# A hybrid decoder kernel: a new order of the first loads, block 0 in two passes, products on zeros, one mixing table

## The reference, cut to what matters

```
h = rmsnorm(x)
[u | v | p | q | gate_logits] = h @ w_in
A: a = gelu(u) * (tril(W_s[g]) @ LN(gelu(v)) + b_s[g])   per chunk of 128 rows, 4 groups g
B: b = scale * groupwise_linear(mean over trailing 2, 4, 8, 16 rows of p, minus p)
C: 4-head attention of q into 256 memory tokens
merged = sig(g_A)*P_A(a) + sig(g_B)*P_B(b) + sig(g_C)*P_C(c);  x += merged @ w_o
x += relu(rmsnorm(x) @ w_up)^2 @ w_down;  final rmsnorm
```

## Time and profile before

| | |
|---|---|
| median of three runs | 967.74 us (967.2 to 967.82) |
| profiled execution, its time | 966.78 us |
| span of its slowest core (core 5) | 965.1 us |
| spans of the eight cores | 962.2 to 965.1 us |
| TensorE busy | 910.6 us, 94% of the span |
| VectorE, ScalarE, GpSimd busy | 383.4, 306.4, 276.8 us |

### The profile page before, as it was taken

How to read it: one execution, slowest core, us unless ns; L and a number is a source line. 1 busy time by engine, 2 the same in 40 slices (tenths; PEclk the granted TensorE clock), 3 DMA queues, 4 the chain that set the end, 5 groups by cost and what they waited for, 6 DMA issues and landing times.

```text
span 965.1 us, 15404 instructions; the slowest of 8 cores (962.2 to 965.1 us)
## 1 busy us (share of the span) xinstructions
PE 910.6 (94%) x5196; PEld 466.3 (48%) x5196; DVE 383.4 (40%) x633; ACT 306.4 (32%) x536; POOL 276.8 (29%) x276
## 2 busy tenths in 40 slices
PE   1599999999999999999999999999999999999996
PEld 0265655444455555554455444554445544455442
DVE  0466665423332233335832244223442234322576
ACT  1254674676322222222333200331003310033332
POOL 1123341623343333442433200232003310033243
PEclk9999999999999999999999999999999999999998
DMA  8627246903284222219570220504114050220134
GB/s 157 182 67 186 87 84 116 175 1 47 43 228 78 44 44 45 44 58 247 98 133 1 48 41 1 88 1 66 22 17 72 1 88 1 39 49 1 45 153 175
DMA packets 34060, 74.14 MB, mean 77 GB/s; under 512 B 19887, under 2 KB 20910, under 8 KB 30144
## 3 DMA queue, kind: packets, MB, share of 16 engines
q0 software_dynamic: 5472, 35.65, 22.2%
q1 hardware_dynamic: 28512, 37.51, 12.5%
HBM read 94.24 MB, written 10.22 MB: 108 GB/s over the span
## 4 chain that ended last, share of the span: by engine, by line
PE 89%; DMA 4%; DVE 2%; ACT 2%; issue 1%; POOL 0%; DVEq 0%; SPq 0%; POOLq 0%; ACTq 0%
PE bank L347 88%; DMA X<-x 3%; DMA CR<-ck 1%; PE bank L350 1%; DVE X L365 1%; ACT X L353 1%; ACT L353 1%; ACT fA L353 0%; DVE stats L562 0%; DVE X L362 0%; POOL stats L356 0%; ACT hT L369 0%; DVEq L128 0%; ACT CR L353 0%; SPq L159 0%
## 5 line engine op out<-in xcount | busy, mean ns | idle before, releaser
L347 PE MATMUL bank<-hT,slot 128*128 128x436 bf16 (+3 forms) x2480 | 466.2, 347 | 4.9 <-DVE hT L371 2.0
L347 PEld LDWEIGHTS bank<-hT,slot 128*128 128x128 bf16 x2480 | 238.9, 98 | 218.6 <-issue 8.7
L347 PE MATMUL bank<-slot,CR 128*128 128x512 bf16 (+1 forms) x1376 | 296.3, 378 | 0.0
L353 ACT ACTIVATE fA<-bank 128x436 f32<-128x436 f32 (+2 forms) x215 | 115.6, 545 | 339.5 <-PE bank L347 329.3
L347 PEld LDWEIGHTS bank<-slot,CR 128*128 128x128 bf16 x1376 | 134.5, 98 | 160.4
L365 DVE SCALAR_TENSOR_TENSOR X<-bank,stats,X 128x512 f32<-128x512 f32 x136 | 102.0, 750 | 119.8 <-PE bank L347 119.8
L353 ACT ACTIVATE fW<-bank 128x436 f32<-128x436 f32 (+2 forms) x103 | 54.7, 534 | 166.3 <-PE bank L347 163.8
L356 POOL TENSOR_TENSOR CR<-fA 128x436 bf16<-128x436 f32 (+1 forms) x69 | 67.5, 980 | 106.9 <-ACT fA L353 102.9
L356 POOL TENSOR_TENSOR stats<-stats,cstt 128x1 f32<-128x1 f32 (+3 forms) x32 | 39.6, 1239 | 136.1 <-DVE stats L362 93.8
L356 DVE TENSOR_TENSOR CR<-fA 128x436 bf16<-128x436 f32 (+1 forms) x51 | 32.7, 645 | 114.6 <-ACT fA L353 114.6
L356 DVE TENSOR_TENSOR fA<-bank,fA 128x436 f32<-128x436 f32 (+1 forms) x77 | 42.7, 603 | 78.4 <-PE bank L347 75.2
(11 more groups left out here) (93 smaller groups left out, 490.6 us busy)
## 6 DMA issues: line engine op xcount, KB each, us to landing
slot<-wpk POOLq DMA_DIRECT2D x30, 1024.0 KB, 13.2
X<-x SPq DMA_DIRECT2D x34, 512.0 KB, 7.5
y<-hT SPq DMA_DIRECT2D x17, 512.0 KB, 2.7
CR<-ck POOLq DMA_DIRECT2D x4, 512.0 KB, 9.9
CR<-cv POOLq DMA_DIRECT2D x4, 512.0 KB, 12.1
CR<-mem SPq DMA_DIRECT2D x2, 512.0 KB, 11.0
gb<-gvec SPq DMA_DIRECT2D x2, 512.0 KB, 10.9
fW<-wst SPq DMA_DIRECT2D x2, 256.0 KB, 10.7
```

What stands on the lines that cost most here:

```text
L347: s.op("pe", lambda e: e.matmul(out, lhsT=lhsT, rhs=rhs, start=start, stop=stop), R_, W_)
L353: s.op("act", lambda e: e.activation(out=out, in_=in_, func=func, **kw), R_, W_)
```

## The change

What it does: (1) constants `onef`, `nhalf`, `qbd`, `ones` are set by VectorE; `nhalf` is no longer loaded. (2) The gain row and the identity are issued by ScalarE's queue; tiles 0 and 1 by SyncE's, tiles 2 and 3 by GpSimd's, ahead of the weights. (3) Chunks v, pq and u are loaded as two halves (k = 0 to 3, k = 4 to 7), each with its own semaphore, one behind the other on GpSimd's queue; u is issued after T(0). (4) `cst` is issued once the second half of v has landed, then the window tables, and the setup loads once the first half of pq has landed; tiles 4 to 7 and 8 to 11 now go through GpSimd's queue. (5) Products on zeros, 6, 5 and 4 of 512 columns, stand in TensorE's list around T(0) and T(1). (6) In block 0 V, P, Q and U are done in two passes, all with k = 0 to 3 and then k = 4 to 7, over open banks. (7) The first of block 1 is reordered, and the rows of tiles 4 to 7 are squared between the products of U(0, g). (8) There is one table CC: the K=1 products are gone, b_s comes broadcast over 128 partitions and is added by VectorE, and the second `setup_mm` is gone.

```diff
+        def load_halves(expect):
+            ...
+            for a in range(2):
+                s.dma("pool", [(slots[sl][:, a * 2048:(a + 1) * 2048], wpk[CH[nm]][:, a * 2048:(a + 1) * 2048])],
+                      writes=[slot_b[sl][a]], owner=slot_b[sl][a])
...
-        norm_load(0, xrow(0))
-        s.dma("sp", [(grow, gvec[0].unsqueeze(0))], writes=grow_b, owner=grow_b[0])
-        load_next("v")
-        load_next("pq")
-        load_next("u")
-        s.dma("sp", [(cstt[:], cst)], writes=[cst_b], owner=cst_b)
-        s.dma("sp", [(bnd[:, B_ID:B_ID + 128], cb[:, B_ID:B_ID + 128])], writes=[ident_b], owner=ident_b)
-        for t in BT[0][1:]:
-            norm_load(t, xrow(t))
-        MEMSET("pool", ones, 1.0, [ones_b])
-        MEMSET("pool", qbd, 0.0, [qbd_b])
+        MEMSET("dve", onef[:], 1.0, [onef_b])
+        MEMSET("dve", nhalf[:], -0.5, [nhalf_b])
+        MEMSET("dve", qbd, 0.0, [qbd_b])
+        MEMSET("dve", ones, 1.0, [ones_b])
+        s.dma("act", [(grow, gvec[0].unsqueeze(0))], writes=grow_b, owner=grow_b[0])
+        s.dma("act", [(bnd[:, B_ID:B_ID + 128], cb[:, B_ID:B_ID + 128])], writes=[ident_b], owner=ident_b)
+        norm_load(0, xrow(0))
+        norm_load(1, xrow(1))
+        norm_load(2, xrow(2), queue="pool")
+        norm_load(3, xrow(3), queue="pool")
+        load_halves("v")
+        load_halves("pq")
+        ACT(tiny[:], onef[0:1, 0:8], AF.Square, [onef_b], [tiny_b])
         for n in range(2):
             bk, bk_b = pb()
...
-            CP("act", gb[:, n * 512:(n + 1) * 512], bk[:, :], [bk_b], [gb_b])
+            CP("dve", gb[:, n * 512:(n + 1) * 512], bk[:, :], [bk_b], [gb_b])
+        def warm(n):
+            bk, bk_b = pb()
+            for _ in range(n):
+                MM(bk[0:64, :], ones, CRf[:, 16384:16896], True, True, [ones_b, qbd_b], [bk_b])
...
-        def setup_mm(i):
+        def setup_mm():
             bk, bk_b = pb()
             for g in range(4):
-                MM(o, bvb[:, g * 128:(g + 1) * 128], wsf[i][:, g, :], True, False, [bvb_b, wsf_b[i]], [bk_b])
-                MM(o, onef, bsrow[:, i * 512 + g * 128:i * 512 + (g + 1) * 128], False, True, bsrow_b + [CC_b[1]], [bk_b])
-            CP("act", CC[i][:].rearrange("p g i -> p (g i)"), bk[:, :], [bk_b], [CC_b[i]])
+                MM(bk[:, g * 128:(g + 1) * 128], bvb[:, g * 128:(g + 1) * 128], wsf[0][:, g, :], True, True, [bvb_b, wsf_b[0]], [bk_b])
+            TT("dve", CC[:].rearrange("p g i -> p (g i)"), bk[:, :], bsb, ALU.add, [bk_b] + bsb_b, [CC_b])
...
-        for i in range(4):
-            nb = norm_a([i])
-            norm_b(*nb)
-            if i >= 1:
-                N(i - 1)
-                T(i - 1)
-        N(3)
-        load_x(BT[1][0:2], after=[slot_b[1]])
-        setup_loads()
-        load_x(BT[1][2:4], after=[slot_b[2]])
-        vmm(0)
-        T(3)
-        for i in range(1, 4):
-            vmm(i)
-        vfin()
-        Q(0)
-        for i in range(4):
-            P(i)
-            vout(i)
-        na = norm_a([4, 5])
-        WIN(0)
...
+        warm(6)
+        ns = [norm_a([i]) for i in range(4)]
+        norm_b(*ns[0])
+        norm_b(*ns[1])
+        N(0)
+        N(1)
+        T(0)
+        warm(5)
+        load_halves("u")
+        norm_b(*ns[2])
+        norm_b(*ns[3])
+        T(1, "act")
+        warm(4)
+        N(2)
+        N(3)
+        vpart(0, 0)
+        vpart(1, 0)
+        T(2, "act")
+        vpart(2, 0)
+        T(3, "act")
+        vpart(3, 0)
+        load_x(BT[1], queue="pool")
+        s.dma("sp", [(cstt[:], cst)], writes=[cst_b], owner=cst_b, after=[slot_b[0][1]])
         s.dma("sp", [(bnd[:, B_CUR:B_SC], cb[:, B_CUR:B_SC])], writes=[bnd_b], owner=bnd_b)
+        setup_loads([slot_b[1][0]])
+        for i in range(4):
+            vmm(i)
+        for i in range(4):
+            P(i, (0,))
+        Q(0, (0,))
+        vfin()
+        for i in range(4):
+            P(i, (1,))
+        Q(0, (1,))
+        for i in range(4):
+            vout(i)
+        WIN(0)
+        for g in range(4):
+            U(0, g, parts=(0,))
+        us, na = [], []
+        for g in range(4):
+            us.append(U(0, g, parts=(1,)))
+            na.append(norm_a([4 + g]))
+        setup_ops(0)
+        for g in range(2):
+            norm_b(*na[g])
+        N(4)
+        setup_mm()
+        MIX(0, 0, *us[0])
+        T(4)
+        N(5)
+        norm_b(*na[2])
+        MIX(0, 1, *us[1])
+        N(6)
+        norm_b(*na[3])
+        MIX(0, 2, *us[2])
+        T(5)
+        MIX(0, 3, *us[3])
+        N(7)
+        vmm, vfin, vout, vpart = V(BT[1])
+        vmm(0)
+        T(6)
+        P(4)
+        vmm(1)
+        T(7)
+        P(5)
+        load_x(BT[2], queue="pool")
+        load_next("kv")
+        mem_loads()
+        wst_load(1)
...
+        vmm(2)
+        P(6)
+        vmm(3)
+        P(7)
+        Q(1)
+        na = norm_a(nx)
         vfin()
         norm_b(*na)
...
         vmm(2)
-        setup_mm(1)
         KV()
```

More of the change, by code:

```diff
@@ L412, in build_program, with norm_load @@
         norm_src = {}
-        def norm_load(t, src, after=()):
+        def norm_load(t, src, after=(), queue="sp"):
             xt, xb = ring("xst", xst, xst_b)
-            s.dma("sp", [(xt, src)], writes=[xb], owner=xb, after=after)
+            s.dma(queue, [(xt, src)], writes=[xb], owner=xb if queue == "sp" else s.buf("xq%d" % t), after=after)
             norm_src[t] = (xt, xb)
@@ L553, in V, with part @@
             gvs = []
+            open_ = {}
+            def part(i, a):
+                t = ts[i]
+                if a == 0:
+                    open_[i] = pb()
+                bk, bk_b = open_[i]
+                for k in range(4 * a, 4 * a + 4):
+                    MM(bk[:, :], hT[:, k, t * 128:(t + 1) * 128], w[:, k, :], k == 0, k == 7, [hT_b[t], wb[a]], [bk_b])
             def mm(i):
[L556 to L559, removed]
+                if i not in open_:
+                    part(i, 0)
+                part(i, 1)
+                bk, bk_b = open_[i]
                 gv, gv_b = tA()
@@ L589, in out, with Q @@
                     pend.append(scale)
-            return mm, fin, out
-        def Q(j):
+            return mm, fin, out, part
+        pq_open = {}
+        def Q(j, parts=(0, 1)):
             w, wb = W("pq", 8)
@@ L597, in Q @@
             for ft in range(2):
-                bk, bk_b = pb()
-                for k in range(8):
-                    MM(bk[:, 0:n], w[:, k, 256 + ft * 128:256 + (ft + 1) * 128], hT[:, k, c0:c1], k == 0, k == 7, htb(j) + [wb], [bk_b])
+                if 0 in parts:
+                    pq_open["q", j, ft] = pb()
+                bk, bk_b = pq_open["q", j, ft]
+                for k in range(4 * parts[0], 4 * parts[-1] + 4):
+                    MM(bk[:, 0:n], w[:, k, 256 + ft * 128:256 + (ft + 1) * 128], hT[:, k, c0:c1], k == 0, k == 7, htb(j) + [wb[k // 4]], [bk_b])
+                if 1 not in parts:
+                    continue
                 if j == 4:
@@ L660, in WIN, with U @@
                 CP("dve", pm[:, ft, c0:c1], bk[:, 0:c1 - c0], [bk_b], [pm_b[ft][j]])
-        def U(j, g, late=False):
+        u_open = {}
+        def U(j, g, late=False, parts=(0, 1)):
             w, wb = W("u", 8)
@@ L665, in U @@
             n = c1 - c0
-            bk, bk_b = pb()
-            for k in range(8):
-                MM(bk[:, 0:n], w[:, k, g * 128:(g + 1) * 128], hT[:, k, c0:c1], k == 0, k == 7, htb(j) + [wb], [bk_b])
+            if 0 in parts:
+                u_open[j, g] = pb()
+            bk, bk_b = u_open[j, g]
+            for k in range(4 * parts[0], 4 * parts[-1] + 4):
+                MM(bk[:, 0:n], w[:, k, g * 128:(g + 1) * 128], hT[:, k, c0:c1], k == 0, k == 7, htb(j) + [wb[k // 4]], [bk_b])
+            if 1 not in parts:
+                return None
             def ge():
@@ L836, in T, with load_x @@
             trans(t, hT, [hT_b[t]], t * 128, eng)
-        def load_x(ts, after=()):
+        def load_x(ts, after=(), queue="sp"):
             for t in ts:
-                norm_load(t, xrow(t), after)
+                norm_load(t, xrow(t), after, queue)
         def N(t):
             norm_c(t, gb[:], gb_b)
-        vmm, vfin, vout = V(BT[0])
+        vmm, vfin, vout, vpart = V(BT[0])
+        warm(6)
+        ns = [norm_a([i]) for i in range(4)]
+        norm_b(*ns[0])
+        norm_b(*ns[1])
@@ L943, in build_program @@
         na = norm_a(nx[0:2])
-        vmm, vfin, vout = V(BT[2])
+        vmm, vfin, vout, vpart = V(BT[2])
         vmm(0)
@@ L1002, in build_program @@
         vt = BT[3] + [16]
-        vmm, vfin, vout = V(vt)
+        vmm, vfin, vout, vpart = V(vt)
         vmm(0)
```

105 lines of the change are left out of this document (41 added, 64 removed).

## The result

The changed kernel takes 944.6 us (median of four runs, 943.5 to 945.0) against 967.5 us for the kernel before (967.1 to 967.8): ratio 0.9761, 95% interval 0.9749 to 0.9772. Forecast were 943.2 us and a range of 937.5 to 951.

What follows compares the result with a forecast made beforehand. TensorE bounds the kernel, busy 94% of the span, with some 32 of its 54 idle us at the start. 22.4 + 0.3 + 3.3 - 1.3 - 1.0 + 0.8 = 24.5; 967.7 - 24.5 = 943.2 us, range 937.5 to 951.

Steps and rivals of the forecast that it cites:

- Arrival of rows: Start loads: tile 0 lands at 5.2 us, all four tiles by about 11, v's halves at 14 and 17.
- End of V: Block 0: V ends at 26.5 us instead of 48.9, gain 22.4 us (18 to 24).
- P, Q, WIN: Block 0 after V: 8.8 us instead of 9.1, gain 0.3 us (-0.5 to 1).
- Tables: Mixing tables: dropping the second whole gains 3.3 us (2 to 3.5); the first loses its K=1 half, 1.65 us.
- Tail of block 0 and the loads: U(0) to U(1): 31.0 us with VectorE's longer list, loss 1.3 us; loads on SyncE charged 1.0 us more.
- The term for the transfers: Tiles 4 to 7 share the engines with SyncE's loads and land close to their squares: loss 1.0 us (0 to 5).
- Block 1: Squares of tiles 8 to 11 leave the gelus, `vout` begins about 1.6 us earlier: gain 0.8 us (-1.5 to 2).
- Products on zeros and two passes: Start: zeros keep TensorE working from 9 to 18 us at no cost; a later clock rise costs 2 to 4 us.
- (b): GpSimd's issue held up by VectorE: tiles 2 and 3 land at 15, V ends at 31 us; 948 us; chance 0.12.
- (a): Loads from 19 us collide: tile 4 or u's second half 5 to 8 us late; 948 to 951 us; chance 0.18.
- (c): Fewer waits in block 0, V ends at 25 us, gain about 29; 938 to 940 us; chance 0.17.
- (d): TensorE's clock stays low over half of blocks 0 and 1, 25 us of work; 968 to 975 us; chance 0.03.

Runs made afterwards that it cites:

- the move of the rows alone: Kernel before, with tiles 1 to 3 ahead of `cst` and the identity on SyncE's queue; 969.6 us, ratio 1.0023.
- yardstick: The changed kernel itself, timed again for comparison with the follow-up kernels; 944.5 us, ratio 0.9761.
- one-pass kernel: Changed kernel, with V, P, Q and U of block 0 each in one go, T(0) to T(3) ahead of V; 942.5 us, ratio 0.9742.
- both with one pass: Changed kernel, memory loads held until tile 7 landed, copies of T(4) to T(7) on ScalarE, block 0's V, P, Q, U unsplit; 942.1 us, ratio 0.9746.
- both changes in the tail: Changed kernel, SyncE's memory loads held until tile 7 has landed and copies of T(4) to T(7) on ScalarE; 943.9 us, ratio 0.9762.

## Why the prediction was right, point by point

- *Arrival of rows.* Right in order. Tile 1 was squared at 8.6 us (said: by 8), all rows by 12.2 us (said: 11). That the queues take turns by packets, read from the earlier trace rows, was shown by the move of the rows alone.
- *End of V.* Said 26.3 to 26.5, measured 26.1 us on core 7; 22.4 us gain forecast, 22.8 measured (48.9 - 26.1).
- *P, Q, WIN.* Said 8.8, measured 34.71 - 26.1 = 8.6 us.
- *Tables.* The second gave its 3.3 us (3.6 in the kernel before with one table), the K=1 products of the first 2.1 instead of 1.65; then 0.8 were lost to the wait for the keys, which I had left out.
- *Tail of block 0 and the loads.* The weakest step. Said 31.0 us, and 1.0 more for the loads, 32.0 in all; measured from U(0) to U(1) 33.9 on core 7 and 31.9 to 32.3 on the seven others. The waits were right: 3.9 idle us forecast, 4.3 measured. (The step's own figures give 29.67 - 1.65 + 2.8 = 30.8, not 31.0.) Where the clock stays up, with the copies on ScalarE and the loads held, the stretch is 30.9 us with the same 4.3 idle us. So the step that failed is the clock in this stretch, which I had priced at nothing: with the wait of 3.1 us for T(5) it falls, and TensorE is busy up to 27.9 us on the seven cores with 3.4 us at the lower level and 29.5 on core 7 with 6.8, for 26.6 us without a fall. N(5) took 2.0 instead of 1.28 us just ahead of that wait, while GpSimd's multiply was running. The term for the transfers was wrong too: held back alone, they change nothing. That seven cores came out at the 32.0 us of the sum is luck: the 1.0 for the loads stands in for the clock.
- *Block 1.* Said 0.8, measured 1.3 us. That its squares would be late on some cores (22.3 us on core 1 of the yardstick, for 20.7) was not foreseen.
- *Products on zeros and two passes.* I priced the zeros at nothing when present and 2 to 4 us when absent; measured 1.8 to 2.1. I took the two passes as useful and gave one pass no price. They cost 2.0 us: when V can start with all four tiles transposed, at 16.5 to 18.5 us, it waits for no weights in the one-pass kernel.
- *Rivals.* (b) said that rows on GpSimd's queue would be starved, after the rule of the Trainium skill (SBUF — State Buffer, section SBUF: two separate sides). By rows, tile 2 is squared at 10.9 us there and at 14.5 us from SyncE's queue, and following the rule's advice for tiles 2 and 3 cost 8 us. VectorE's clearing was under way from 1.5 to 2.4 us; what little it may have delayed is not seen, so no run here shows the starving itself. (a), loads that collide, did not come: ScalarE waits 2.1 and 3.0 us for the rows of tiles 6 and 7, and nothing is gained when it doesn't. (c) did not come either: V ended at 26.1 us, not 25. (d), a clock that stays low, was real as a mechanism, but not as 25 us of work: in the changed kernel 3.4 to 6.8 us pass at the lower level after the first rise, and up to 24 us (core 4) where the rows come late.

The errors had both signs: +0.4, +0.2, +0.5, -1.9 and -0.8 for the steps above, +0.3 for the part behind the first product of S, which core 7 here does faster than core 5 before. The sum came out 1.4 us from the time, in part because they offset one another. The mechanism of the large term, the start, was right; the closeness of the number is partly luck.

## What to carry to other kernels

At the start count each queue's packets in order, not its bytes: a small table behind large cast transfers costs what they cost, so issue rows before weights and make constants on the chip (together with the new block 1 worth 18 us here; not tested apart). A break in the products is charged twice, once as the wait and once as the clock that may fall behind it. Here 4.3 us of waits went with 27.9 us of busy time when one of them was 3.1 us long, and with 26.6 when none was over 1.7. So keep the first long run unbroken rather than begin it early with half the operands, and test filler products against exactly that version. When a part is sped up on all cores and the time stays, look at the slowest core's next stretches, and at where its clock falls now.

## What the runs showed of the hardware

- The clock at a start differs by core: with the same program it rose at 9.9 to 15.6 us over the eight cores of the changed kernel, and in the run with tiles 2 and 3 on SyncE's queue it stayed up on two cores and fell for 3.4 to 17 us on six, which spread the spans from 943.5 to 951.2 us.
- From the first product of S to the end the same instructions take 840.5 us on some cores and more on others: up to 841.9 in the trace of the changed kernel, up to 843.9 in that of both with one pass. It is why a gain of 1 to 2 us on most cores need not show in the slowest. One part is the fall of the clock near 100 us: with both changes in the tail the five cores that have it take 841.9 to 842.6 us, the three others 840.5 to 841.7. What makes the rest was not tested.
- The f32 products of the second table were followed by a fall of the clock on five of eight cores near 115 us; in the kernel before with one table none falls there. But such products are not needed for a fall: with both changes in the tail, and no second table, five cores fall near 100 us, behind two waits.
